# Mixture-of-experts down products: high and low part of the 48-row block in one stationary operand, and the next rows loaded block by block

## The reference

```
combine = ...                       # router: two of 16 experts for each position
for e in range(N_EXPERTS):          # 16
    h = silu(t @ w_gate[e]) * (t @ w_up[e])      # 1024 -> 256
    y = y + combine[:, e:e + 1] * (h @ w_down[e])  # 256 -> 1024
x = layer_norm(DEEPNORM_ALPHA * x + y)
```

## Time and profile before

| | us |
|---|---|
| median of 3 runs | 981.41 (980.06 to 983.18) |
| the profiled execution | 976.16 |
| its span, first to last instruction | 974.4 |
| expert steps, first gate product to the end | 690 to 974 |

### The profile page before, as it was taken

One profiled execution on the slowest core, in us unless ns is written; L12 is line 12 of the kernel. 1 busy time (PEld: TensorE's weight loads), 2 busy tenths in 40 slices (PEclk: granted clock), 3 DMA queues, 4 the chain that ended last, 5 costly groups with the idle time before them and its releaser, 6 DMA issues. The chain is left out here.

```text
span 974.4 us, 15658 instructions
## 1 busy us (share of the span) xinstructions
PE 940.6 (97%) x5655; PEld 797.9 (82%) x5655; DVE 590.8 (61%) x1263; ACT 350.9 (36%) x737; POOL 193.4 (20%) x256
## 2 busy tenths in 40 slices
PE   7999999999999999999999999999899999999994
PEld 6899888777768888888867888879789898989883
DVE  6744341588676776756665445568353567777675
ACT  6123031345574555400025333230322334444441
POOL 0013100112241120013210000005200233342344
PEclk9999999999998999999999999999999999999998
DMA  8122010001699501700223000045888988899972
GB/s 308 63 87 87 1 66 1 1 1 51 259 412 368 174 23 34 277 15 1 87 86 134 1 1 1 1 173 218 272 278 261 316 276 296 294 323 328 316 254 81
DMA packets 67278, 151.60 MB, mean 156 GB/s; under 512 B 8720, under 2 KB 16144, under 8 KB 67216
## 3 DMA queue, kind: packets, MB, share of 16 engines
q1 hardware_dynamic: 59920, 133.82, 39.4%
q0 software_dynamic: 7296, 16.95, 4.5%
HBM read 107.62 MB, written 52.03 MB: 164 GB/s over the span
## 5 line engine op out<-in xcount | busy, mean ns | idle before, releaser
L2001 PEld LDWEIGHTS h_ps<-xgT,e_gate_up 128*128 128x128 f32 x1024 | 155.6, 192 | 4.9 <-issue 2.6
L2001 PE MATMUL h_ps<-xgT,e_gate_up 128*128 128x176 f32 x1024 | 157.1, 315 | 2.5 <-DVEq L2109 2.5
L265 PE MATMUL unit_ps<-whi,xhi 128*128 128x512 f32 (+1 forms) x256 | 97.8, 382 | 6.1 <-DVE wlo L303 6.1
L267 PE MATMUL unit_ps<-whi,xlo 128*128 128x512 f32 (+1 forms) x256 | 97.5, 381 | 0.0
L266 PE MATMUL unit_ps<-wlo,xhi 128*128 128x512 f32 (+1 forms) x256 | 97.5, 381 | 0.0
L265 PEld LDWEIGHTS unit_ps<-whi,xhi 128*128 128x128 f32 x256 | 48.4, 189 | 14.1 <-DVE xlo L347 6.0
L2144 DVE SCALAR_TENSOR_TENSOR z<-y_ps,slot_weight,x_rows 128x512 f32<-128x512 f32 (+1 forms) x64 | 45.7, 746 | 22.2 <-PE y_ps L2015 22.1
L267 PEld LDWEIGHTS unit_ps<-whi,xlo 128*128 128x128 f32 x256 | 48.3, 189 | 7.7
L266 PEld LDWEIGHTS unit_ps<-wlo,xhi 128*128 128x128 f32 x256 | 48.4, 189 | 7.5
L2013 PE MATMUL y_ps<-e_dn_hi,h_hi 128*128 128x512 f32 (+1 forms) x128 | 51.9, 405 | 0.0
L2015 PE MATMUL y_ps<-e_dn_hi,h_lo 128*128 128x512 f32 (+1 forms) x128 | 50.2, 392 | 0.0
(11 more groups left out here) (346 smaller groups left out, 2133.3 us busy)
## 6 DMA issues: line engine op xcount, KB each, us to landing
e_gate_up<-w_gu SPq DMA_DIRECT2D x16, 2048.0 KB, 10.3
e_down_raw<-w_dn SPq DMA_DIRECT2D x16, 1024.0 KB, 6.2
slot_rows<-zeros SPq DMA_DIRECT2D x22, 522.0 KB, 6.2
slot_sums<-zeros SPq DMA_DIRECT2D x22, 512.0 KB, 6.3
x_rows<-slot_rows SPq DMA_DIRECT2D x16, 522.0 KB, 4.8
slot_sums<-z SPq DMA_DIRECT2D x16, 512.0 KB, 4.4
wraw<-w_in SPq DMA_DIRECT2D x24, 256.0 KB, 4.8
xraw<-xT SPq DMA_DIRECT2D x16, 256.0 KB, 5.0
```

Of the source, the lines that this page charges most:

```text
L265: pe.matmul(o, hi, whi[:, s, 0:w], start=(s == 0), stop=False)
L267: last = pe.matmul(o, lo, whi[:, s, 0:w], start=False, stop=(s == KD - 1))
L2001: end = pe.matmul(hps[:, m, gu * CAP:(gu + 1) * CAP], gate_up[:, b, s, w], xT[:, s, :], start=(s == 0), stop=(s == KD - 1))
```

## The change

The 48-row block of h no longer has its low part in `h_lo`. The tile `h_hi` grows to 240 columns: 128 of block 0, 48 of block 1 (high), 16 of zero, and 48 of block 1 (low). A stationary operand of 112 columns (48 high, 16 zero, 48 low) gives both products with the high weights at once, in PSUM partitions 0 to 47 and 64 to 111. Each of the units 2 and 3 so takes two products in place of three for each f. DVE makes the low part in two instructions (128 columns and 48), and adds up the two PSUM parts in two instructions in place of one, the second of which waits for the first. SP loads a block of the next rows as soon as that block's z is made, ahead of the store of z.

```
-                for u, free in ((0, 4), (1, 2), (2, 3)):
-                    pe.wait_ge(z_made, n(4, free))
-                    down(u, 0)
+                pe.wait_ge(z_made, n(4, 4))
+                down(0, 0)
+                down(1, 0)
+                pe.wait_ge(small_lo_done, n(2, 1))
+                small_down(0, 0)
                 pe.wait_ge(hlo_done, n(2, 2))
-                for u in range(3):
-                    down(u, 1).then_inc(ysum, 1)
+                down(0, 1).then_inc(ysum, 1)
+                down(1, 1).then_inc(ysum, 1)
+                pe.wait_ge(small_lo_done, n(2, 2))
+                small_down(0, 1).then_inc(ysum, 1)
                 pe.wait_ge(z_made, n(4, 5))
-                down(3, 0)
-                down(3, 1).then_inc(ysum, 1)
+                small_down(1, 0)
+                small_down(1, 1).then_inc(ysum, 1)
...
+                def small_down(j, f):
+
+                    w, bank = 2 * f + j, BANK[2 + j]
+                    if f:
+                        pe.matmul(yps[0:B1, bank, :], hhi[:, f, P:CAP], dn_lo[:, b, w, :], start=False, stop=False)
+                    last = pe.matmul(yps[0:64 + B1, bank, :], hhi[:, f, P:LOW + B1], dn_hi[:, b, w, :], start=(f == 0), stop=(f == 1))
+                    if f == 0:
+                        last = pe.matmul(yps[0:B1, bank, :], hhi[:, f, P:CAP], dn_lo[:, b, w, :], start=False, stop=False)
+                    return last
...
-                    dve.tensor_tensor(hlo[:, m, :], hh[:, m, :], hhi[:, m, :].bitcast(f32), ALU.subtract).then_inc(hlo_done, 1)
+                    dve.tensor_tensor(hlo[:, m, :], hh[:, m, 0:P], hhi[:, m, 0:P].bitcast(f32), ALU.subtract).then_inc(hlo_done, 1)
+                    dve.tensor_tensor(hhi[:, m, LOW:LOW + B1], hh[:, m, P:CAP], hhi[:, m, P:CAP].bitcast(f32), ALU.subtract)\
+                       .then_inc(small_lo_done, 1)
...
-                    dve.scalar_tensor_tensor(z[c][:, f], yps[r, BANK[u], :], wgt[r, b, c:c + 1], rows[b][r, c, f], ALU.mult, ALU.add,
+                    rest = rows[b][r, c, f]
+                    if c:
+                        dve.scalar_tensor_tensor(z[c][:, f], yps[64:64 + B1, BANK[u], :], wgt[r, b, c:c + 1], rest, ALU.mult, ALU.add)\
+                           .then_inc(half_made, 1)
+                        dve.wait_ge(half_made, n(2, j + 1))
+                        rest = z[c][:, f]
+                    dve.scalar_tensor_tensor(z[c][:, f], yps[r, BANK[u], :], wgt[r, b, c:c + 1], rest, ALU.mult, ALU.add,
                                              accum_out=zsum[r, c, j:j + 1]).then_inc(z_made, 1)
...
+                hold(placed_at, n(1, 1))
                 for c in range(2):
                     hold(z_made, n(4, 2 * c + 6))
+                    if not is_one_of_last(e, 2):
+                        fetch(n(CAP, 2 * CAP), b, [c])
                     sp.dma_start(k.z_dram[bass.ds(n(CAP, c * P), ROWS[c]), :], z[c][:]).then_inc(z_stored, 16)
-                if not is_one_of_last(e, 2):
-                    hold(placed_at, n(1, 1))
-                    fetch(n(CAP, 2 * CAP), b)
```

More of the change, by code:

```diff
@@ L1810, in experts @@
     act_g = at("silu_g", 144.5, [P, 2, CAP])
-    hhi = at("h_hi", 146, [P, 2, CAP], f32r)
-    hlo = at("h_lo", 147.5, [P, 2, CAP], f32r)
+    LOW = P + 64
+    hhi = at("h_hi", 150, [P, 2, LOW + B1], f32r)
+    hlo = at("h_lo", 147.5, [P, 2, P], f32r)
     slot_id = at("slot_number", 149, [P, NE, 2])
@@ L1832, in experts @@
     gsum, silu, hmul, hhi_done, hlo_done = k.sem("gu_sum"), k.sem("silu_done"), k.sem("h_mul"), k.sem("hhi_done"), k.sem("hlo_done")
+    small_lo_done, half_made = k.sem("small_lo_done"), k.sem("half_made")
     ysum, z_made, z_stored, held, held_sp = (k.sem(x) for x in ("y_sum", "z_made", "z_stored", "held", "held_sp"))
@@ L1873, in hold, with fetch @@
                 sp.sem_inc(held_sp, 1)
-            def fetch(row, b):
-                for c in range(2):
+            def fetch(row, b, blocks=range(2)):
+                for c in blocks:
                     sp.dma_start(rows[b][0:ROWS[c], c, :], k.xs_dram[bass.ds(row + c * P, ROWS[c]), :]).then_inc(rows_loaded[b], 16)
@@ L2006, in step, with down @@
                     turn(1 - b, h(32, 32 * (1 + b)))
-                def down(u, f):
-                    c, j = UNITS[u]
+                def down(j, f):
                     w = 2 * f + j
-                    hi, lo = (t[:, f, c * P:c * P + ROWS[c]] for t in (hhi, hlo))
-                    out = yps[0:ROWS[c], BANK[u], :]
+                    hi, lo, out = hhi[:, f, 0:P], hlo[:, f, :], yps[:, BANK[j], :]
                     pe.matmul(out, hi, dn_hi[:, b, w, :], start=(f == 0), stop=False)
@@ L2043, in _ @@
             act.sem_inc(ysum, 8)
-            act.wait_ge(stats_cleared, 6)
+            act.wait_ge(stats_cleared, 7)
             act.wait_ge(dn_loaded, 16)
@@ L2054, in step @@
                     act.wait_ge(ysum, n(4, 8))
-                    act.activation(hhi[:, m, :], hh[:, m, :], ACT.Copy).then_inc(hhi_done, 1)
+                    act.activation(hhi[:, m, 0:CAP], hh[:, m, :], ACT.Copy).then_inc(hhi_done, 1)
                 if not last:
@@ L2114, in _ @@
             dve.memset(rs[:], 1.0).then_inc(stats_cleared, 1)
+            dve.memset(hhi[:, :, CAP:LOW].bitcast(f32), 0.0).then_inc(stats_cleared, 1)
             for c in range(2):
                 dve.memset(tmp[c][:], 0.0).then_inc(stats_cleared, 1)
-            dve.wait_ge(stats_cleared, 6)
+            dve.wait_ge(stats_cleared, 7)
             split_down(0, lambda a, c: c)
```

## The result

The changed kernel takes 993.06 us (median of 3 runs, 990.74 to 995.65) where the kernel before takes 981.41: a ratio of 1.0123 with a 95% interval of 1.0098 to 1.0147. It is slower, as forecast, but by 11.7 us where 6.3 were forecast, and it lies 1 us outside the range. The profiled execution took 990.74 us with a span of 989.0, so 14.6 more than the span before.

A forecast was written before the change was run, and what follows sets the result against it. PE was taken to bind by 0.24 us over the DVE and POOL loop. Terms -3.16, -1.12, +7.28, +1.62 and +1.7 gave +6.3 us: 987.7 us, 0.65% slower than the median 981.41; range 978 to 992.

The forecast's parts named there:

- the cover: The 0.24 us by which PE's step (16.75 us) exceeded the DVE and POOL loop (16.51); forecast to be gone.
- the loop through POOL: Once a step, `ln_out`, `e_dn_lo`, held `slot_weight` copy, gathers, root, next `ln_out`: 16.51 us before, 17.66 forecast.
- PE: Four fewer down products a step at 0.23 us each: gain 0.79 in steps 0 to 3, 0.56 in 4 and 5.
- D: Start of a step's first down product on PE; distance forecast 16.0 us in steps 0 to 3, 16.2 in 4 and 5.
- X: Start of `ln_out` on DVE; forecast at D + 0.17 where PE alone binds, 1.64 behind D in step 14.
- DVE: Two added 48 x 512 instructions a step, 0.85 us each with the wait; `e_dn_lo` ends at X + 12.45, not X + 11.30.
- The held turn: POOL held to the end of `e_dn_lo`: turns of 17.66 us, a loss of 0.91 in each of steps 6 to 13.
- SP: Row loads ahead of stores cost about half a us, unwaited for; down weights asked for 1.2 us later, costing nothing.
- The last steps: X of step 14 late: +1.62 us; both added DVE instructions in the last step: +1.7; nothing else moves there.
- POOL gets in early: Rival: writes land early or POOL gets in before `e_dn_lo`, PE binds throughout; -7.5 us, 973.9 us; chance 0.10.
- Half and half: Rival: every second copy on POOL gets in, two steps take 17.66 + 16.19; -0.2 us, 981.2 us; chance 0.12.
- The hold lasts one instruction only: Rival: DVE holds POOL's copy for one `e_dn_lo`, turn of 16.6 us; -3.2 us, 978.2 us; chance 0.07.

The follow-up runs named there:

- e3: The changed kernel without the second DVE instruction, which adds the upper PSUM part (one product left out of the result): 972.15 us, ratio 0.9922.
- e4: The kernel before with the second DVE instruction and its wait put in, adding the 48-row block's product a second time: 996.3 us, ratio 1.0185.
- e6: The changed kernel with POOL's wait for landed writes moved behind the gathers and the slot numbers made in two instructions: 966.32 us, ratio 0.9878.
- e7: The kernel before with POOL's wait for landed writes moved behind the gathers, slot numbers made in two instructions: 978.27 us, ratio 0.9996.
- e5: The changed kernel with SP's load of the next gate weights held until the gathers have landed: 985.58 us, ratio 1.0076.
- e9: The changed kernel with DVE waiting for its own result and filling one column behind each `e_dn_lo`: 984.94 us, ratio 1.0052.
- e1: The changed kernel with the row loads on SP back behind both stores of z, as before: 991.52 us, ratio 1.0118.

## Why the prediction was right, and where it was wrong

**The direction, right, for the reason given.** PE was the bound by 0.24 us, DVE's two instructions took the cover away, and the loop through POOL became the bound. e3 and e4 show the two instructions, e6 against the change and e7 the loop.

**PE, right.** The distance of D was 15.92 to 15.94 us in steps 0 to 3 (16.0 forecast) and 16.00 and 15.93 in steps 4 and 5 (16.2). From the first down product to that of step 5 the kernel gained 4.1 us (83.79 less 79.71), where 3.7 were forecast. In steps 4 and 5 X had been taken at D + 0.17, with 0.15 for the second low part of h; it stood at D + 0.05 (771.67 against 771.62), which is about half of what these steps were shorter.

**DVE, right.** The added instructions stand in the timeline as 883.85, 884.64, 885.42 and 886.21: 0.79 from the first of a pair to the second and 0.78 to the next pair, where 0.85 was taken. The operand in the upper partitions cost nothing extra that the row shows.

**The held turn, right in size, wrong in number.** It was forecast at 17.66 and took 17.73 to 17.76 us (787.66 to 805.39, 879.42 to 897.18, 914.73 to 932.49). But the step "from the second round on the step lasts 17.66" said that every turn is held. `ln_out` waited for the root at the end of five of these turns, and once more in the last step. Of the five, three took these 17.7 us; the ones that end at 842.02 and 860.66 took 17.43 and 18.64.

**The failed step: the turns in between, and what PE's stall brings with it.** Under *SP* the gate load has no term at all. The trace of before had it 1.03 us behind the second gather (887.58 against 886.55). The gathers move 1.15 us back with `e_dn_lo`, while the load hangs on PE and does not move, so that the forecast's own term was enough to turn their order round. In the held turns it now stands ahead of the second gather, and z waited 1.26 to 2.11 us for rows, five times. The late z costs in two ways. It moves `ln_tmp` and `e_dn_lo` back, to whose end POOL is held: `e_dn_lo` of the turn from 860.66 ended 13.72 us behind `ln_out` (874.38), where 12.45 was forecast, and the two turns from 842.02 to 879.42 took 18.64 and 18.76 us. In other pairs this does not show: that from 879.42 to 914.73 takes 35.31 us, against 2 x 17.66 = 35.32, by luck, since a held turn of 17.76 is followed by one that PE, and not the loop, makes 17.55. And it makes the stall on PE longer, from the forecast 1.8 us to between 2.48 and 3.61, and in three of five cases the clock went to its lower level afterwards.

The steps from D of step 6 (803.55) to that of step 14 (952.00) took 148.45 us, 7.17 more than 8 x 17.66. Of that some 3.3 are the clock, by the estimate above; 1.8 is a shift (`ln_out` stood 1.84 behind D in step 6 and 0.05 in step 14), which the next paragraph gives back; and the remaining 2.1 are turns longer than 17.66 for the late rows. e5 and e6 show the chain from the other end: with the load held back the rows were late twice instead of five times, and with POOL's order changed no gathered row came late, no clock fell in the steps, and no step took over 16.63 us. That the late rows lead to the long stall is shown by the rows; what part of the loss is the clock's no run shows by itself.

**The last steps, wrong by 1.7 us in the other direction.** X of step 14 was taken as 1.64 behind its D; it stood 0.05 behind (952.05 against 952.00), because the turn before it was one bound by z and PE, not a held one. From D of step 14 to the end the kernel lost 1.6 us, not 3.3. But what else moves there was taken as nothing, and that was wrong too: the slot numbers were held once more (3.56 us at 961.10), `ln_out` waited 3.72 us for the root at 969.36, PE waited 3.33 us for the `h_lo` behind it, and the first `z` stood 6.65 us behind D (972.83 - 966.18) instead of 3.20. From the first `z` to the last it took 5.72 us instead of 3.47. Against these 5.7 us stand 0.85 gained from D of step 14 to that of 15 and 3.2 in the branch at the end. That the total came out near the forecast is luck.

**Ahead of the experts.** 3.4 us of the profiled difference lie ahead of the first down product (707.91 against 704.49), in code that is the same in both but for one clearing of 0.09 us. In the runs of the experiments that place stood between 703.17 (e9) and 706.79 (e1), in no order that follows the change. So it varies from execution to execution; why is not shown. The forecast has no term for it, and the medians, 11.7 us apart, hold less of it than the spans, 14.6 apart.

Put together: the sum of +6.3, less 0.6 for the first six steps, plus 7.2 in the loop, less 1.7 at the end, gives +11.2, which is what the trace has from the first down product to the end (281.1 against 269.9 us).

**The rivals.** *POOL gets in early* did not occur as a rule. *Half and half* is near to what the timeline shows: the copy got through in four of ten turns (0.18 to 0.23 us), and `ln_out` waited for nothing in four of the nine turns from 787.66 on. But its price was wrong: it took a turn that is not held as bound by PE at 16.19. The turn behind a held one takes 17.55 us or more, since the late rows of the held turn, and then the clock, have made PE late. *The hold lasts one instruction only* falls by the changed kernel's own rows and by e9. The slot numbers at 870.92 stood through the end of `ln_tmp` and all of `e_dn_lo`:

```profile
869.50 2.47 DVE L2119 SCALAR_TENSOR_TENSOR ln_tmp<-z,z_neg_mean,ln_g 128x1024 f32<-128x1024 f32 x2
870.92 3.56 POOL L1923 TENSOR_SCALAR slot_ids<-slot_where 128x4 int32<-128x4 f32 x1
871.90 2.48 DVE L2093 TENSOR_TENSOR e_dn_lo<-e_down_raw,e_dn_hi 128x512 fp32r<-128x512 f32 x4
```

They ended at 874.48, 0.10 behind the last `e_dn_lo` (871.90 + 2.48), not behind the instruction of DVE's that was under way at 870.92. The Trainium skill, SBUF — State Buffer, section "SBUF: two separate sides", words the lock as one for "the whole instruction". By that rule the slot numbers would have ended with the second `ln_tmp`, near 872.0; this trace does not agree with it.

## What to carry to other kernels

Where one engine is the bound by a quarter of a microsecond, a saving on it must be costed together with the loop that takes over, and every transfer that hangs on the engine that did not move must be set against those that did: a load that used to follow a gather may now lead it. A stall of TensorE can cost more than its length, since the products behind it may run at the lower clock: in these traces that happened behind waits of 2.02 us (e5) and more, though not behind every one. So cost a stall twice, with the clock and without, and ask whether another engine is late by as much, which hides it. Compare the ends of two traces as well: 3.2 us between these kernels lie in one branch. When a change loses time in a wait, look for work that stands behind that wait without needing it: splitting the slot numbers in two turned a loss of 1.2% into a gain of 1.2%.

## What the runs showed of the hardware

- A GpSimd instruction that reads SBUF was held through a run of two-input VectorE instructions standing back to back: 3.56 us for the slot numbers (normally 0.24) and 4.54 us for a gather's issue at 816.05 (normally 1.14). In e9, with a wait and a one-column write between them, the VectorE instructions started 0.72 to 0.82 us apart instead of 0.60, and that was enough to let it in.
- TensorE's granted clock fell to between 0.52 and 0.55 for some 3.4 us behind waits of 2.48 and 3.19 us, and stayed at 1.00 behind others of 2.51 and 3.21. The shortest such wait in any trace was 2.02 us (e5, clock 0.66 over the next 3.4 us).
- A 2 MB load asked for 0.17 to 0.79 us ahead of the second of two gathers (128 and 48 rows) went with rows that came 1.26 to 2.11 us too late; with the load held back (e5) there were only two such waits, of 0.9 us each.
- The branch with which TensorE leaves the block took 3.41 to 3.61 us in the traces of three kernels and 0.37 to 0.38 in those of ten.
